# A hybrid decoder layer on one core: the eight samples of its recurrent heads in 32 rows per head, the next tile's first projection among the last samples, and new orders where attention begins and ends

## What is computed

```python
p = rms_norm(x, norm_w) @ w_in                     # one projection; q|k|v|gate for attention, q|f|i|gate for HGRN2
att = sliding_window_attention(qa, ka, va, sinks)  # window 128, 8 query heads, 2 key heads, meta tokens always visible
# HGRN2, 4 heads of 128 x 128 state, per token:
f = lb + (1 - lb) * sigmoid(z);  k = (1 - lb) * sigmoid(-z)
S_t = diag(f_t) @ S_{t-1} + outer(k_t, v_t);       o_t = S_t.T @ silu(q_t)
x = x + concat(att * silu(ga), rms_norm_head(o) * silu(gh)) @ w_out
```

## Time and profile before

| what | us |
|---|---|
| median of three runs | 1118.86 |
| lowest and highest of them | 1117.51, 1123.49 |
| the profiled execution, own time | 1119.97 |
| its span in the trace | 1118.2 |
| PE busy in the span | 1093.1 |

### The profile page before, as it was taken

The page is one execution under the profiler, slowest core; times in us unless marked ns, Lnnn a source line. Parts: engine busy times, 40 slices in busy tenths (PEclk is TensorE's granted clock), DMA queues, the critical chain, the costliest instruction groups (busy, mean ns, idle before and its releaser), DMA issues.

```text
span 1118.2 us, 25609 instructions
## 1 busy us (share of the span) xinstructions
PE 1093.1 (98%) x9277; PEld 901.0 (81%) x9277; DVE 722.1 (65%) x1873; ACT 441.6 (39%) x1265; POOL 332.6 (30%) x404
## 2 busy tenths in 40 slices
PE   6999999999999999999999999999999999999998
PEld 4877888888888888888877888888888887788887
DVE  6867666666676766666876666566666776754453
ACT  6522212222222222223425556655666665532330
POOL 0013333333333333333531221122112226532331
PEclk9999999999999999999999999999999999999999
DMA  6742011111111110114523511111121134434431
GB/s 205 249 142 96 35 64 66 66 66 56 66 66 66 66 66 35 40 49 173 200 64 130 189 56 61 71 47 56 64 69 48 58 124 160 166 136 147 166 115 77
DMA packets 49390, 108.32 MB, mean 97 GB/s; under 512 B 5088, under 2 KB 17888, under 8 KB 49312
## 3 DMA queue, kind: packets, MB, share of 16 engines
q1 hardware_dynamic: 49328, 107.51, 27.1%
HBM read 70.23 MB, written 38.26 MB: 97 GB/s over the span
## 4 chain that ended last, share of the span: by engine, by line
PE 87%; DVE 5%; DMA 3%; ACT 2%; issue 2%; SPq 0%; POOL 0%; ACTq 0%; DVEq 0%
PE h_bank_a L967 5%; PE h_bank_b L967 5%; PE h_bank_b L969 5%; PE h_bank_a L968 5%; PE h_bank_a L969 5%; PE h_bank_b L968 5%; PE o_bank L2694 5%; PE o_bank L2696 5%; PE o_bank L2695 5%; PE h_bank_t L953 3%; PE a_bank_o L2022 3%; PE a_bank_b L1971 3%; PE a_bank_a L1971 3%; PE a_bank_a L1973 3%; PE a_bank_b L1973 3%; PE a_bank_a L1972 3%
## 5 line engine op out<-in xcount | busy, mean ns | idle before, releaser
L967 PE MATMUL h_bank_b<-h_w_hi,h_h_hi 128*128 128x512 f32 x256 | 106.4, 416 | 1.2 <-DVE h_g L617 1.2
L967 PE MATMUL h_bank_a<-h_w_hi,h_h_hi 128*128 128x512 f32 x256 | 103.1, 403 | 0.0
L969 PE MATMUL h_bank_b<-h_w_hi,h_h_lo 128*128 128x512 f32 x256 | 101.0, 395 | 0.0
L968 PE MATMUL h_bank_b<-h_w_lo,h_h_hi 128*128 128x512 f32 x256 | 100.4, 392 | 0.0
L969 PE MATMUL h_bank_a<-h_w_hi,h_h_lo 128*128 128x512 f32 x256 | 99.9, 390 | 0.0
L968 PE MATMUL h_bank_a<-h_w_lo,h_h_hi 128*128 128x512 f32 x256 | 99.9, 390 | 0.0
L1755 DVE CUSTOM_DVE_ANT_0 a_sm<-a_sc,a_hidden,a_neg_sink 128x272 f32<-128x272 f32 x128 | 57.6, 488 | 58.2 <-PE a_sc L1999 58.2
L1552 ACT ACTIVATE a_prb<-a_sm,a_neg_m 128x256 f32<-128x256 f32 x128 | 64.3, 503 | 41.0 <-DVE a_neg_m L1755 39.2
L1971 PE MATMUL a_bank_a<-a_w_hi,a_h_hi 128*128 128x512 f32 (+1 forms) x208 | 77.9, 375 | 0.4 <-DMA a_h_lo<-h_split 0.4
L1971 PE MATMUL a_bank_b<-a_w_hi,a_h_hi 128*128 128x512 f32 (+1 forms) x200 | 75.5, 377 | 0.0
L1973 PE MATMUL a_bank_a<-a_w_hi,a_h_lo 128*128 128x512 f32 (+1 forms) x208 | 73.6, 354 | 0.0
(11 more groups left out here) (335 smaller groups left out, 3017.2 us busy)
## 6 DMA issues: line engine op xcount, KB each, us to landing
h_split<-h_h_hi SPq DMA_DIRECT2D x17, 512.0 KB, 3.0
h_split<-h_h_lo SPq DMA_DIRECT2D x17, 512.0 KB, 3.8
a_h_hi<-h_split SPq DMA_DIRECT2D x17, 512.0 KB, 3.5
a_h_lo<-h_split SPq DMA_DIRECT2D x17, 512.0 KB, 4.4
h_x<-x_prompt SPq DMA_DIRECT2D x16, 512.0 KB, 3.3
o_m<-mixed SPq DMA_DIRECT2D x16, 512.0 KB, 4.0
o_x<-x_prompt SPq DMA_DIRECT2D x16, 512.0 KB, 4.2
y_prompt<-o_x SPq DMA_DIRECT2D x16, 512.0 KB, 2.6
```

Source lines behind the costliest of these rows:

```text
L967: pe.matmul(out[:, :], h_hi[t.slot][:, k, :], hi, start=(k == 0), stop=False)
L968: pe.matmul(out[:, :], h_hi[t.slot][:, k, :], lo, start=False, stop=False)
L969: ins = pe.matmul(out[:, :], h_lo[t.slot][:, k, :], hi, start=False, stop=(k == KT - 1))
```

## The change

In the samples: a head's output goes to 32 rows of its own (head h in rows 32h to 32h + 31, 128 columns), so `qm` has 32 columns per sample, one square and one mix instruction serve all four heads, and the gates of the samples are first copied to the same rows (`sample_gates`). SP's order becomes one store ahead of each reload. PE takes tile 2's first projection, in two halves, between the outputs of samples 4, 5 and 6. DVE takes `g_mul` of tile 0, `x_var`, `x_scale` and the two `split_low` of tile 2 one to two samples later, and the block totals ahead of the samples' mix. Where attention begins: PE runs the first half of tile 1's gate projection ahead of `outputs`; DVE normalises tile 1's queries ahead of HGRN2's second-last mix; `turn_k` and the second half of tile 2's gate projection come ahead of `values`. In the loop and at its end `place_q` and `q_rest` of a tile stand at the end of the iteration before: the instruction order stays the same on ACT inside the loop; in the written-out iterations they now precede the output stage's weight splits.

```diff
             for b in range(NS):
                 sp.wait_ge(s1_done, b + 1)
                 sp.dma_start(by_key(new_state_sample[b]), by_head(ring[b % 4])).then_inc(s1_stored[b % 4], 16)
-                if b + 4 < NS:
-                    sp.wait_ge(s1_stored[b % 4], 16)
-                    sp.wait_ge(so_mm, b + 1)
-                    sp.dma_start(by_head(ring[b % 4]), by_key(state[b + 4])).then_inc(st_loaded[b % 4], 16)
+                if 1 <= b < NS - 3:
+                    sp.wait_ge(s1_stored[b - 1], 16)
+                    sp.wait_ge(so_mm, b)
+                    sp.dma_start(by_head(ring[b - 1]), by_key(state[b + 3])).then_inc(st_loaded[b - 1], 16)
...
+            def sample_gates():
+                dve.wait_ge(g_done, 1)
+                for h in range(HH):
+                    ins = dve.tensor_copy(g_q[32 * h:32 * h + 32, :], G[0][SROW:SROW + 32, h * P:(h + 1) * P])
+                ins.then_inc(s_placed, 1)
+
+            def sample_mix():
+                dve.wait_ge(orstd_done, 1)
+                dve.wait_ge(s_placed, 2)
+                dve.scalar_tensor_tensor(mix_q, bank_o[:, 0:P], orstd[:, 0:1], g_q, ALU.mult, ALU.mult).then_inc(mix_done, 1)
...
             sample_state(0)
-            g_mul(tile(0, 0))
-            x_var(tile(0, 2))
             for b in range(1, NS):
                 if b + 1 < NS:
                     sample_key(b + 1)
+                if b == 6:
+                    split_low(tile(0, 2), 1)
                 sample_state(b)
                 if b == 1:
+                    g_mul(tile(0, 0))
+                elif b == 2:
+                    x_var(tile(0, 2))
+                elif b == 3:
                     x_scale(tile(0, 2))
-                elif b in (3, 5):
-                    split_low(tile(0, 2), (b - 3) // 2)
+                    sample_gates()
+                elif b == 4:
+                    split_low(tile(0, 2), 0)
             fk_affine(tile(0, 1))
             dve.wait_ge(o_mm, 1)
             dve.wait_ge(fk_done, 2)
             q_levels(tile(0, 1), 0, 1)
             o_var(0)
-            mix(0, G[0], MIX_S, 64)
+            block_totals(tile(0, 1))
+            sample_mix()
...
                 for h in range(HH):
-                    ins = pe.matmul(bank_o[0:64, h * P:(h + 1) * P], qm[:, h, 64 * b:64 * b + 64], ring[b % 4][:, h * P:(h + 1) * P],
-                                    start=(b == 0 and h == 0), stop=(b == NS - 1), skip_group_check=True)
+                    ins = pe.matmul(bank_o[32 * h:32 * h + 32, 0:P], qm[:, h, 32 * b:32 * b + 32], ring[b % 4][:, h * P:(h + 1) * P],
+                                    start=(b == 0), stop=(b == NS - 1), skip_group_check=True)
...
             sample_output(2)
+            sample_outer(4)
             turn_x(t2, 0)
-            for b in range(4, NS):
-                sample_outer(b)
-                sample_output(b - 1)
-                if b == 5:
-                    pe.wait_ge(h_low, 5)
-                    turn_x(t2, 1)
+            sample_output(3)
+            sample_outer(5)
+            pe.wait_ge(h_low, 5)
+            turn_x(t2, 1)
+            sample_output(4)
+            sample_outer(6)
+            pe.wait_ge(v_copied, 2)
+            project(t2, bank_a, 0, (0,))
+            sample_output(5)
+            sample_outer(7)
             pe.wait_ge(h_low, 6)
+            project(t2, bank_a, 0, (1,)).then_inc(f_proj, 1)
+            sample_output(6)
             turn(bank_t, z_nat, zt)
             sample_output(NS - 1)
...
             turn_p(t1, 1)
+            pe.wait_ge(q_placed, 2)
+            turn_k(t2)
+            project(t2, kv_bank(t2), 2, range(4, 8)).then_inc(g_proj, 1)
             values(t1, 0)
-            project(t2, kv_bank(t2), 2, range(4, 8)).then_inc(g_proj, 1)
             scores(t1, 3)
             turn_p(t1, 2)
-            pe.wait_ge(q_placed, 2)
-            turn_k(t2)
```

More of the change, by code:

```diff
@@ L455, in k_copy, with square_o @@
                 act.activation(KN[:, :], bank_t[:, :], ACT.Copy).then_inc(k_nat, 1)
-            def square_o(n, rows=P):
+            def square_o(n):
                 act.wait_ge(o_mm, n + 1)
@@ L460, in square_o @@
                 wait(act, o_squared, n)
-                for h in range(HH):
-                    ins = act.activation(junk_o[0:rows, h * P:(h + 1) * P], bank_o[0:rows, h * P:(h + 1) * P], ACT.Square,
-                                         accum_out=oss[0:rows, h:h + 1])
+                for h in range(1 if isinstance(n, int) and n == 0 else HH):
+                    ins = act.activation(junk_o[:, h * P:(h + 1) * P], bank_o[:, h * P:(h + 1) * P], ACT.Square,
+                                         accum_out=oss[:, h:h + 1])
                 ins.then_inc(o_squared, 1)
@@ L725, in o_var, with mix @@
                 dve.tensor_scalar(ovar[:, :], oss[:, :], 1.0 / P, EPS, ALU.mult, ALU.add).then_inc(ovar_done, 1)
-            def mix(n, g, out, rows):
+            def mix(n, g, out):
                 dve.wait_ge(orstd_done, n + 1)
@@ L732, in mix @@
                     c = slice(h * P, (h + 1) * P)
-                    ins = dve.scalar_tensor_tensor(out[0:rows, c], bank_o[0:rows, c], orstd[0:rows, h:h + 1], g[0:rows, c],
-                                                   ALU.mult, ALU.mult)
+                    ins = dve.scalar_tensor_tensor(out[:, c], bank_o[:, c], orstd[:, h:h + 1], g[:, c], ALU.mult, ALU.mult)
                 ins.then_inc(mix_done, 1)
+            def sample_gates():
+                dve.wait_ge(g_done, 1)
+                for h in range(HH):
+                    ins = dve.tensor_copy(g_q[32 * h:32 * h + 32, :], G[0][SROW:SROW + 32, h * P:(h + 1) * P])
[4 more added lines that the diff above has]
+                dve.scalar_tensor_tensor(mix_q, bank_o[:, 0:P], orstd[:, 0:1], g_q, ALU.mult, ALU.mult).then_inc(mix_done, 1)
             def split_weights(c, chunks=range(KT)):
@@ L872, in iteration @@
                     wait(dve, mix_stored, 16 * last.n)
-                    mix(last.n, G[last.slot], MIX[last.slot], P)
+                    mix(last.n, G[last.slot], MIX[last.slot])
                 if ahead:
@@ L907, in vector @@
             wait(dve, mix_stored, 16 * gone.n)
-            mix(gone.n, G[gone.slot], MIX[gone.slot], P)
+            mix(gone.n, G[gone.slot], MIX[gone.slot])
             q_levels(before, 3, 4)
@@ L937, in vector @@
             wait(dve, mix_stored, 16 * before.n)
-            mix(before.n, G[before.slot], MIX[before.slot], P)
+            mix(before.n, G[before.slot], MIX[before.slot])
             near_mask(last, 1)
@@ L1115, in iteration @@
             def iteration(t0, t1, t2, last, tail=True, ahead=True, more=True):
-                if ahead:
+                if ahead and tail:
                     pe.wait_ge(v_copied, t0.n + 1)
@@ L1609, in iteration @@
             def iteration(t0, t1, t2, last, tail=True, ahead=True, more=True):
-                place_q(t0)
                 gate(t0)
@@ L1624, in iteration @@
                 sink_exp(t0)
+                place_q(t1)
             t0, t1 = tile(0, 1), tile(0, 2)
@@ L1633, in scalar @@
             exps(t0, 2)
+            place_k(t1)
             place_p(t0, 2)
-            place_k(t1)
             exps(t0, 3)
             sink_exp(t0)
+            place_q(t1)
             with act.Fori(*LOOP) as it:
@@ L1819, in vector @@
             split_weights(2, range(4, 8))
+            q_norm(tile(0, 1))
             yield
-            q_norm(tile(0, 1))
             gate_plus(tile(0, 0))
@@ L1880, in vector @@
             gate_mul(t0)
+            q_rest(t1)
             def iteration(t0, t1, t2, last, mask, tail=True, ahead=True, more=True):
@@ L1884, in iteration @@
                     denominators(last)
-                q_rest(t0)
                 gate_plus(t0)
@@ L2976, in _ @@
             pe.wait_ge(attention.sems["k_placed"], 2)
+            next(a)
             next(h)
```

30 lines of the change are left out of this document (17 added, 13 removed).

## The result

The changed kernel takes 1120.99 us (median of 22 runs, 1119.01 to 1123.48), the kernel before 1119.23 (22 runs, 1116.79 to 1123.49). The ratio is 1.0019, with an interval of 1.0012 to 1.0026: some 2 us slower, where 2.2 us faster was forecast, and outside the range. The profiled execution took 1120.02 us with a span of 1118.2, by accident the same span as before. It had reached the start of tile 1's last projection, ahead of which PE's list has no edit, at 50.72 instead of 52.08; in the profiles of all kernels here, changed or not, that start lies between 50.5 and 52.8, so the difference is the run's.

What follows compares the result with a forecast made beforehand. PE was taken to bound the kernel, busy 1093.1 of 1118.2 us, with SP's queue setting the samples' pace. Terms -1.1 + 3.3 + 1.2 - 1.2 gave 2.2 us, hence 1116.5 us, range 1111.5 to 1120.0.

Steps and rivals of the forecast that it cites:

- The samples without the clock: Sample stage at full clock: earlier reloads and shorter outputs let PE go on at 83.9 instead of 86.21, +2.3 us.
- the 0.27 of the row: Lower bound for a sample output, 0.27 us, from the profile's 128*32 group, which streams as many columns.
- The estimate of 0.43: Sample output time if four column tiles do no better than three: 1.02 / 2.38 = 0.43 us; the forecast took 0.4.
- an idle of 2.0 us at 64.4: Samples: PE, done with outer product 5, was to wait 2.0 us for tile 2's x until 66.4.
- The cover that is gone: Samples: with tile 2's projection moved, PE idles 5.5 us behind and 2.0 at 64.4; clock loss 1.7 each, -3.4 us.
- a sign of being wrong: Listed under what would show the forecast wrong: a half-clock stretch of more than 5 us.
- The slower rival: PE at half clock through the sample stage; samples lose 8 to 9 us, total -5, 1123.8 us; chance 0.08.
- Where attention begins: Gate projection fills the wait at outputs, clock kept (+1.7), key turn 3.35 us earlier; +3.3 us, bounds 1.6 and 3.35.
- Entry of attention's loop: Waits for place_p (0.7) and turn_q (0.8) go, last probabilities' turn about 0.3 late: +1.2 us, range 0 to 1.5.
- The written-out iterations: place_q ahead of weight splits delays values by 0.23 in four iterations, 0.3 in one: -1.2 us, bounds -1.9 and +1.0.
- room before the maxima: Inside attention's loop, DVE's q_rest moves past denominators with time to spare: 0 us.
- The sum: Whole kernel: -1.1 + 3.3 + 1.2 - 1.2 = 2.2 us faster, forecast 1116.5 us.

Runs made afterwards that it cites:

- e1: Kernel before with only the samples' part of the change, attention and launch order as before: 1120.42 us, ratio 1.0018.
- e5: Changed kernel with tile 2's first projection put back whole behind the samples, behind the turn of q: 1116.10 us, ratio 0.9967.
- e9: e5 with 64-row sample outputs as in the kernel before, the changed orders on SP, DVE and PE kept: 1116.29 us, ratio 0.9986.
- e14: Changed kernel with tile 2's projection behind the samples, written-out place_q and q_rest behind splits, entry q_rest behind the samples' gate product, and 64-row outputs: 1109.69 us.
- e13: Kernel before with only the 32-row sample outputs and what they need, all orders old: 1120.57 us, ratio 1.0014.
- e15: Kernel before with one edit, DVE's q_rest ahead of denominators in attention's iterations: 1115.28 us, ratio 0.9965.
- e4: Changed kernel with tile 2's q_rest at the entry of attention's loop moved behind the samples' gate product on DVE: 1120.27 us, ratio 1.0001.
- e16: Kernel before with the attention part, written-out place_q and q_rest behind the weight splits, entry q_rest behind the samples' gate product: 1114.29 us, ratio 0.9947.
- e8: Changed kernel with SP's old order at the samples (store, wait, reload, next store): 1121.29 us, ratio 1.0013.
- e12: Changed kernel with the three mends of e14 but 32-row outputs, and DVE's gate product of tile 1 ahead of totals and mix: 1109.39 us.

## Why the prediction was wrong, step by step

Two steps failed: the charge for the clock at the samples, in its mechanism, and the entry of attention's loop, which is the largest miss in size. A third, the written-out iterations, was mis-sized.

**The samples without the clock: right in sum.** +2.3 was forecast; e1 has 3.3 less full-clock time than before (1111.9 to 1108.6). An output measured 0.35, between the 0.4 taken and the 0.27 of the row, and 2.9 times as fast as the old form's 1.02. The estimate of 0.43, worked out from the 2.38 of the Trainium skill (TensorE: Matmul & The Clock Gate, Part 3: Packing small matmuls), was too slow. But the sum hid two large terms of opposite sign: the outputs 5.6 to 6.7, and the projection among the samples -4.4 (e5, 1110.3 to 1105.9 at full clock). The forecast had the projection's 5.6 us on PE's path, behind an idle of 2.0 us at 64.4 that did not come (PE had no wait between 50.72 and its turn of z), and never set it against leaving the projection where it was.

**"The cover that is gone": the step whose mechanism failed.** I charged the clock, 1.7 twice, to the two idle times. The idle behind the samples came as forecast (5.6 us against 5.5), the one at 64.4 did not. From 79 to 89, that is in the idle behind the samples and after it, the changed kernel's profile runs at half clock and loses 5.1: a stretch of more than 5 us, which the prediction itself named as a sign of being wrong. But the idle is not the main cause: without it (e5) the clock is 0.993 all the same, and with 64 rows and no such idle (e9, e14) it is 0.998 to 0.999. The narrow outputs, with what belongs to them, lower it, also by themselves (e13), by 5.9 to 7.3 us of work, more than the 3.4 charged. The Trainium skill (TensorE: Matmul & The Clock Gate, HAM oscillation) tells of a clock that falls when PE waits for data. The 2.8 us wait ahead of `outputs` agrees with it: the four profiles that have it (before, e1, e13, e15) lose 1.3 to 1.7 us in 565 to 575, and without it the others lose nothing there. The stretches at 52 and 60 have no wait ahead of them. The cost of the change's best-looking edit was thus put on another edit, and too small. Over all runs the clock costs the change 4 us net (0.9955 to 0.9919), where -3.4 at the samples and +1.7 where attention begins, -1.7 net, were forecast. The slower rival (half clock through the sample stage, 0.08) had the effect, through another cause and at less than half of its size.

**Where attention begins: right**, +3.3 of +3.3; the wait of 2.8 went to 0.6, and the stretch at 569 went with it. No stretch below 0.99 is left there in the changed kernel's profile.

**Entry of attention's loop: the largest miss, 1.7.** +1.2 was forecast, -0.5 measured. What the step counted, `place_p` and the bank of `turn_q`, came: up to the loop's first `turn_q` it gained 1.1 (26.10 to 24.96). The first iteration then lost 1.7 (22.89 to 24.55). The step had overlooked that DVE's `q_rest`, moved to the end of the entry, passes the product of the samples' rows, for which ACT's gate copy waits. e4 shows it: with that order put right the iteration takes 23.05.

**The written-out iterations: right mechanism, mis-sized.** -1.2 forecast, -2.1 measured: 0.36 in the first and 0.42 to 0.49 in the others, instead of 0.23 and 0.3. I had taken the first iteration's 5.01 from `turn_q` to `values` for all; the next three take 4.87 to 4.89 before, and ACT needs 5.37 in the changed kernel. That half of the edit, `q_rest` ahead of `denominators`, is worth 3.1 by itself (e15), I did not see, since I put it at 0 with "room before the maxima", while the wait that mattered was that of `scores`.

**The sum.** Forecast +2.2, measured -2.1 by the ratio: 0.8 too good at the samples, 1.7 at the entry, 0.9 in the iterations, by marks of one profile. The remaining 0.9 stays open, since marks of one profile each cannot settle it. That the samples missed by only 0.8 is in part luck: the work came out 1.0 better than forecast (3.3 against 2.3), and the clock took 5.3 (e1, 0.9955 to 0.9908) instead of 3.4.

## What to carry to other kernels

When an edit shortens PE's work, read the mean granted clock over many runs beside the time, since what the work gains the clock can take back whole, and multiply span by clock to see the two apart. It works both ways: the new orders at the samples gained some 4 us, most of it by a higher clock (e16 to e14). When a step moves on an engine, list every instruction that it passes and ask who waits for each of them: the two surprises of the attention part, one bad and one good, were small instructions that `q_rest` had passed. And a projection moved to fill one wait uncovers another; it was worth 5 us to leave it where it covered the gates.

## What the runs showed of the hardware

PE's clock falls without any wait ahead of it: in the changed kernel PE was busy from 20 to 76, and still the granted clock was 0.50 in 52 to 54 and in 60 to 62. The levels are 1.2 and 2.4 GHz, and each stretch lost 1.7 us, or a multiple of it (5.1 at 79 to 90). Ahead of the first of them stand outer products of 8 rows and half a projection, and no output yet (the first comes at 55.15); e9, with 64 rows, has a stretch at the same place (51 to 54), and e4, e5, e8 and e12, with 32 rows, have none there, so that one is not the outputs'. Ahead of the second stand outputs of 32 columns, outer products and the start of a projection. With PE busy 10 of 10 us, e5 ran at 0.74 in 60 to 70 and e9 at 1.00; they differ in the sample outputs and what belongs to them (the masked query, the squares, the mix). Why the chip answers to that shape was not tried.
